# Decode attention of an MLA layer: scores in four 32-column strips over two key groups, and a new order of scoring and summing

## The chip, the cores and the metric

The kernel runs on one core of one Trainium2 chip. The metric is the device time of one execution in microseconds (us). The kernel before took 1875.65 us as the median of three runs (1873.12, 1875.65 and 2126.9). The execution that the profiler recorded took 1877.48 us, with a span of 1875.5 us.

## What is computed

One inference step of a two-layer decoder trunk. Layer 0 mixes tokens by multi-head latent attention (MLA), layer 1 by dilated sliding windows; each is followed by a squared-ReLU MLP. There are 512 prompt tokens and 8 samples (decode) with one new token each. The change touches only the MLA attention of the samples:

```python
# per sample: 16 heads, 4096 past keys in 32 pages, a latent of 256 and a rotary key of 32 each
ckv_past = ckv_pool[page_table].reshape(B, past, 256)
kpe_past = kpe_pool[page_table].reshape(B, past, 32)
q_lat = einsum("bthn,chn->bthc", q_nope, w_uk)
s_past = einsum("bthc,bkc->bhtk", q_lat, ckv_past) + einsum("bthr,bkr->bhtk", q_pe, kpe_past)
s_new  = einsum("bthc,bkc->bhtk", q_lat, c_kv) + einsum("bthr,bkr->bhtk", q_pe, k_pe)
p = softmax(concatenate([s_past, s_new]) * 96 ** -0.5)
o_lat = einsum("bhtk,bkc->bthc", p[..., :past], ckv_past) + einsum("bhtk,bkc->bthc", p[..., past:], c_kv)
o = einsum("bthc,chv->bthv", o_lat, w_uv) @ w_o      # after this the residual and the MLP
```

## The kernel before, in words

The program is written by hand, one instruction stream for each engine, tied by counting semaphores. Each engine takes its instructions strictly in the written order, so a wait holds back all that stands behind it. `dve.wait_ge` and the like are such waits; `link` makes VectorE wait for its own last result.

**Gathering.** The 4096 past keys of a sample are NG = 4 groups of 1024 keys. GpSimd fetches each with two indirect DMAs (L1941 the latents, 1 MB; L1942 the rotary keys), row p of a group holding 8 consecutive keys. The buffer `gat` has GR = 8 places, two samples. From group n = 8 on, the issue waits for `group_summed >= n - 7`: the same place must have been used by the sum of two samples earlier.

**Turning.** `turn_group` (L1311): VectorE transposes a group in blocks of 32x32 into `KT`, which has KR = 3 slots. A slot is free when the group that held it has been scored.

**Scores.** In a turned group, partitions 32i to 32i+31 hold 32 latent components of the keys of partition block i. `score_group` (L660, L661) multiplies with `qbd`, a block-diagonal weight matrix of 128x128 for each of 8 latent slices and the rotary slice: block i holds the 16 heads in the first 16 of its 32 columns, the rest are zeros. Nine matmuls of 256 columns give 128 x 256 scores of one group; two PSUM banks hold a sample's four groups. ScalarE fills `qbd` for two samples ahead (`spread_queries`, L1759, L1760).

**Softmax.** `key_max` (L1316 to L1322): VectorE reduces 128x1024 scores, brings the four blocks' maxima to partitions 0 to 31, takes the maximum with the new token's score and writes the bias for all blocks. ScalarE takes the exponentials with their row sums (L1771). `turn_probs` (L1330) turns 128x1024 probabilities back into blocks of 32 columns.

**Sums.** `sum_keys` (L671): 32 matmuls with 32 probability columns as weights, in turn in four column strips of the array (`r = 32 * (c % 4)`), 256 latent columns moving; the four strips' partial sums lie in four partition blocks. ScalarE copies them (L1779), `sum_rows` and `weights` make the denominators, `turn_latent` (L688, L689) adds the strips, divides and transposes, `latent_out` adds the new token.

**Order.** TensorE, for b = 0 to 8: score groups 0 and 1 of sample b; sum and row sums of b-1; score groups 2 and 3 of b; turn_latent of b-1. VectorE in each round: maximum of b-1, turn group 2 of b, turn the probabilities of b-1, turn groups 3 of b and 0 of b+1, weights of b-1, turn group 1 of b+1, latent of b-1. After the last sample TensorE multiplies with `w_uv` (L710), and the output projection with `w_omla` follows in four chunks, each split into a high and a low part by ScalarE (L1640) and GpSimd (L1901). The first two chunks are already in their raw buffer `wraw` during the decode attention; `KT` and `qbd0` lie in the place of the split buffer `whl`. SP issues all plain DMAs: `w_uv` waits for the seventh sum (`group_summed >= 28`).

## Time and profile before

| | before |
|---|---|
| profiled execution | 1877.48 us, span 1875.5 us |
| TensorE busy in the span | 1627.6 us (87%) |
| VectorE, ScalarE, GpSimd busy | 741.7, 450.1, 615.5 us |
| granted TensorE clock, mean of the span | 0.907 |
| first turned key group, first output projection | 390.17 us, 589.78 us |

"Busy" counts the time in which an engine works on an instruction; queue and semaphore instructions are left out. Matmul spans overlap, so a busy TensorE is not one at its peak. PEclk is the clock granted to TensorE as a share of 2.4 GHz: 0.50 is 1.2 GHz. A float32 matmul shows as two instructions. In brackets behind a row stands the idle time before it and who ended it. Idle time of an engine off the critical path costs nothing.

### The profile page before, as it was taken

How to read it: one execution, taken by the hardware profiler on the slowest of the kernel's cores; microseconds unless marked ns; L12 is line 12 of the kernel's file. 1: busy time of each engine (PE TensorE's matmuls, PEld its weight loads, DVE VectorE, ACT ScalarE, POOL GpSimd, SP SyncE). 2: the span in 40 equal slices, each digit the busy share in tenths (PEclk: the TensorE clock that was granted, in tenths of full speed). 3: DMA queues.
4: the chain of work that ended last, by engine and by line, in shares of the span. 5: the costliest groups of instructions: out<-in, count | busy, mean ns of one | idle time of the engine just before them, and what ended most of it. 6: DMA issues, size and time to landing. Idle time of an engine off the chain costs nothing.

```text
span 1875.5 us, 28456 instructions
## 1 busy us (share of the span) xinstructions
PE 1627.6 (87%) x12089; PEld 1514.2 (81%) x12089; DVE 741.7 (40%) x1156; ACT 450.1 (24%) x822; POOL 615.5 (33%) x277
## 2 busy tenths in 40 slices
PE   4657888679996999999999999998667999999995
PEld 3646666567776999999999999997545999999994
DVE  5355565366662542014312266313445641024114
ACT  3203343321112322112222111112432321122220
POOL 1311110313322464346533343221001464356440
PEclk8867788779998999999999999987876999999997
DMA  4125420235551453444433446445910453444221
GB/s 132 64 97 198 153 68 23 92 133 210 221 198 46 135 179 135 161 153 157 157 113 138 162 162 220 166 156 178 312 72 0 135 179 134 151 156 154 102 67 45
DMA packets 123259, 258.52 MB, mean 138 GB/s; under 512 B 7032, under 2 KB 104456, under 8 KB 116832
## 3 DMA queue, kind: packets, MB, share of 16 engines
q1 hardware_dynamic: 117024, 219.47, 34.3%
q0 software_dynamic: 6144, 37.75, 5.3%
q8 instruction: 68, 1.11, 0.2%
q14 instruction: 23, 0.19, 0.0%
HBM read 249.61 MB, written 95.58 MB: 184 GB/s over the span
## 4 chain that ended last, share of the span: by engine, by line
PE 73%; DVE 16%; DMA 3%; issue 2%; ACT 2%; POOL 2%; SPq 1%; ACTq 0%; DVEq 0%; POOLq 0%
PE ps L438 19%; PE ps L442 18%; PE ps L439 18%; PE ps L660 4%; PE ps L671 2%; DVE KT L1311 1%; PE ps L587 1%; PE ps L605 1%; DMA dv<-in_state 1%; PE ps L864 1%; DVE sq L1434 1%; PE ps L787 1%; DVE mxs L1261 1%; PE ps L830 1%; PE ps L661 1%
## 5 line engine op out<-in xcount | busy, mean ns | idle before, releaser
L1901 POOL TENSOR_TENSOR whl<-wraw,whl 128x2048 fp32r<-128x2048 f32 (+3 forms) x127 | 448.3, 3539 | 728.8 <-ACT whl L1640 728.7
L438 PE MATMUL ps<-hA,whl 128*128 128x260 f32 x1344 | 372.6, 296 | 43.0 <-POOL hA L1901 15.6
L439 PE MATMUL ps<-hA,whl 128*128 128x260 f32 x1344 | 365.8, 292 | 0.0
L1640 ACT ACTIVATE whl<-wraw 128x2048 fp32r<-128x2048 f32 (+3 forms) x127 | 185.9, 1487 | 499.0 <-PE ps L442 410.3
L438 PEld LDWEIGHTS ps<-hA,whl 128*128 128x128 f32 x1344 | 267.0, 199 | 46.7 <-POOL hA L1901 17.3
L438 PE MATMUL ps<-uT,whl 128*128 128x260 f32 x1024 | 273.5, 288 | 16.8 <-POOL uT L1901 16.8
L442 PE MATMUL ps<-hA,whl 128*128 128x260 f32 x1344 | 281.5, 292 | 0.0
L439 PE MATMUL ps<-uT,whl 128*128 128x260 f32 x1024 | 271.0, 285 | 0.0
L439 PEld LDWEIGHTS ps<-hA,whl 128*128 128x128 f32 x1344 | 267.7, 199 | 0.1
L442 PEld LDWEIGHTS ps<-hA,whl 128*128 128x128 f32 x1344 | 217.3, 198 | 0.0
L438 PEld LDWEIGHTS ps<-uT,whl 128*128 128x128 f32 x1024 | 196.9, 192 | 17.6 <-issue 17.6
L442 PE MATMUL ps<-uT,whl 128*128 128x260 f32 x1024 | 210.1, 287 | 0.0
L439 PEld LDWEIGHTS ps<-uT,whl 128*128 128x128 f32 x1024 | 197.3, 193 | 0.0
L1379 DVE TENSOR_TENSOR xT<-xT,ps 128x520 f32<-128x520 f32 (+1 forms) x48 | 33.4, 696 | 391.6 <-PE ps L442 391.3
L438 PE MATMUL ps<-hB,whl 128*128 128x260 f32 x640 | 168.8, 285 | 0.0
L439 PE MATMUL ps<-hB,whl 128*128 128x260 f32 x640 | 166.6, 282 | 0.0
L442 PEld LDWEIGHTS ps<-uT,whl 128*128 128x128 f32 x1024 | 160.4, 192 | 0.0
L442 PE MATMUL ps<-hB,whl 128*128 128x260 f32 x640 | 129.9, 285 | 0.0
L1901 POOL TENSOR_TENSOR uT<-tmp,uT 128x520 f32 x64 | 84.0, 1313 | 133.9 <-ACT uT L1650 133.9
L660 PE MATMUL ps<-KT,qbd 128*128 128x256 f32 x512 | 120.1, 389 | 9.0 <-DVE KT L1311 9.0
L1398 DVE SCALAR_TENSOR_TENSOR tmp<-ps,rstd 128x520 f32<-128x520 f32 x64 | 44.8, 700 | 199.8 <-PE ps L442 195.0
L439 PEld LDWEIGHTS ps<-hB,whl 128*128 128x128 f32 x640 | 121.6, 190 | 0.1
(255 smaller groups left out, 2139.6 us busy)
## 6 DMA issues: line engine op xcount, KB each, us to landing
out_ds<-in_state SPq DMA_DIRECT2D x32, 2047.0 KB, 10.5
wraw<-in_w_up SPq DMA_DIRECT2D x32, 1024.0 KB, 5.6
wraw<-in_w_down SPq DMA_DIRECT2D x32, 1024.0 KB, 5.1
wraw<-in_w_qkv SPq DMA_DIRECT2D x18, 1024.0 KB, 7.0
out_ds<-in_state SPq DMA_DIRECT2D x8, 2044.0 KB, 13.2
dv<-in_state SPq DMA_DIRECT2D x36, 256.0 KB, 5.8
dv<-q_scratch SPq DMA_DIRECT2D x6, 1024.0 KB, 7.3
wraw<-in_w_omla SPq DMA_DIRECT2D x4, 1024.0 KB, 5.4
```

The costliest lines, as they stand in the source:

```text
L438: pe.matmul(ps[:, 2 * u + a, 0:HALF], hi(k), rhs(k, 0)[:, c], start=first, stop=False)
L439: pe.matmul(ps[:, 2 * u + a, 0:HALF], hi(k), rhs(k, 1)[:, c], start=False, stop=False)
L442: ins = pe.matmul(ps[:, 2 * u + a, 0:HALF], lo(k), rhs(k, 0)[:, c], start=False, stop=last)
L587: pe.matmul(ps[:, i % 2, 0:(t + 1) * P], qh[:, h % 4, tok], kh[:, h % 4, 0:(t + 1) * P], start=True, stop=True).then_inc(scores_ready, 1)
L605: ins = pe.matmul(ps[:, 4 + i % 2, 0:VD], pT[:, i % 2, b * P:(b + 1) * P], v[:, b, h * VD:(h + 1) * VD], start=(b == 0), stop=(b == t))
L660: pe.matmul(out, qbd[b % 2][:, j, :], kt[:, :, j, :], start=(j == 0), stop=False)
L661: pe.matmul(out, qbd[b % 2][:, 8, :], KT[:, n % KR, KPP * KVL:], start=False, stop=True).then_inc(keys_scored, 1)
L671: ins = pe.matmul(ps[r:r + 32, 4 + b % 2, 0:KVL], pturn[:, c * 32:(c + 1) * 32], gat[:, n % GR, (c % KPP) * KVL:(c % KPP + 1) * KVL], star ...
L1379: free(dve.tensor_tensor(cols(xT, f), cols(xT, f), zt(u), ALU.add))
L1398: free(dve.scalar_tensor_tensor(out=out, in0=zt(u), scalar=0.0, in1=rooted(u), op0=ALU.max, op1=ALU.mult))
L1640: ins = act.activation(dst(0), src, ACT.Copy)
L1901: return pool.tensor_tensor(dst, src, hi.bitcast(F32), ALU.subtract)
```

## The change

- Scores of two groups are taken together: `qbd` has two stationary blocks of 32 columns for each slice (strip 0: heads of partition blocks 0 and 1, strip 1: of 2 and 3, 16 columns each); group g's strips go to partitions 64g and 64g+32. 36 matmuls a pair, one PSUM bank for a sample (128x512).
- The maximum runs over 128x512 and then over two halves of 16 heads, with two 32x32 transposes.
- The probabilities are turned 128x512 wide, and four ScalarE copies place them with zeros between them in `pfin`, from which the sums read as before.
- KR = 4: the fourth slot for turned keys is the first raw weight buffer `wraw[:, 0]` with a piece of `rstd`. The second `w_omla` chunk, which lay there, is loaded after all pairs are scored.
- A new order on TensorE, VectorE and ScalarE. The gathers on GpSimd and their waits are unchanged (GR = 8).

```diff
-KR = 3
+KR = 4
-        KT = sb("KT", [P, KR, GW], F32, cx)
-        qbd0 = sb("qbd0", [P, 9, P], F32, cx)
+        KT = sb("KT", [P, KR - 1, GW], F32, cx)
+        qbd = [sb(f"qbd{i}", [P, 9, 2, 32], F32, cx) for i in range(2)]
...
+        NB = 2 * KPP * 32
+        pexp = flat[:, 0:NB]
+        pturn = flat[:, NB:2 * NB]
+        pfin = flat[:, 2 * NB:4 * NB]
+        def keyT(n):
+            if n % KR < KR - 1:
+                return KT[:, n % KR, 0:KPP * KVL], KT[:, n % KR, KPP * KVL:]
+            return wraw[:, 0, :], rstd[:, T - KPP * ROPE:]
... TensorE
-            def score_group(n):
...
+            def score_pair(b, pair):
+                if pair == 0:
                     pe.wait_ge(queries_spread, b + 1)
                     if b >= 2:
                         pe.wait_ge(keys_exp, b - 1)
+                n0 = b * NG + 2 * pair
+                pe.wait_ge(keys_turned, n0 + 2)
+                for j in range(9):
+                    for g in range(2):
+                        ckv_, kpe_ = keyT(n0 + g)
+                        moving = ckv_.rearrange("p (s j q) -> p s j q", s=KPP, j=8)[:, :, j, :] if j < 8 else kpe_
+                        for st in range(2):
+                            r = 32 * (2 * g + st)
+                            ins = pe.matmul(ps[r:r + 32, b % 2, 256 * pair:256 * pair + 256], qbd[b % 2][:, j, st, :], moving,
+                                            start=(j == 0), stop=(j == 8), skip_group_check=True)
+                ins.then_inc(pairs_scored, 1)
             def sum_keys(b):
-                pe.wait_ge(probs_turned, b + 1)
+                pe.wait_ge(probs_placed, b + 1)
...
+            score_pair(0, 0)
+            score_pair(0, 1)
             for b in range(NS + 1):
-                if b < NS:
-                    score_group(NG * b)
-                    score_group(NG * b + 1)
                 if b:
                     sum_keys(b - 1)
                     sum_rows(b - 1)
-                if b < NS:
-                    score_group(NG * b + 2)
-                    score_group(NG * b + 3)
+                if b < NS - 1:
+                    score_pair(b + 1, 0)
+                    score_pair(b + 1, 1)
                 if b:
                     turn_latent(b - 1)
... SP
-            chunk((0, (KC, MC), wsrc(io["w_omla"], 0, KC, MC, MC)))
...
             sp.wait_ge(group_summed, NG * (NS - 1))
             sp.dma_start(wuv, wsrc(io["w_uv"], 0, 2, 0, H * VD)).then_inc(wuv_in, 16)
+            sp.wait_ge(pairs_scored, NS * NG // 2)
+            chunk((0, (KC, MC), wsrc(io["w_omla"], 0, KC, MC, MC)))
... VectorE
-            dve.memset(qbd0[:], 0.0)
-            dve.memset(qbd1[:], 0.0)
+            for t in (*qbd, mcol, mtop):
+                dve.memset(t[:], 0.0)
...
+            dve.memset(pfin, 0.0)
...
             def turn_group(n):
-                if due(n - KR + 1):
-                    dve.wait_ge(keys_scored, n - KR + 1)
+                if n >= KR:
+                    dve.wait_ge(pairs_scored, (n - KR) // 2 + 1)
+                elif n == KR - 1:
+                    dve.wait_ge(chunk_low, 5 + H // 2)
                 dve.wait_ge(gather_in[n % GR], 32 * (n // GR + 1))
-                dve.transpose(KT[:, n % KR, :], gat[:, n % GR, :]).then_inc(keys_turned, 1)
+                if n % KR < KR - 1:
+                    dve.transpose(KT[:, n % KR, :], gat[:, n % GR, :]).then_inc(keys_turned, 1)
+                else:
+                    ckv_, kpe_ = keyT(n)
+                    dve.transpose(ckv_, gat[:, n % GR, 0:KPP * KVL])
+                    dve.transpose(kpe_, gat[:, n % GR, KPP * KVL:]).then_inc(keys_turned, 1)
             def key_max(b):
...
-                link(dve.tensor_reduce(mall[:], mq[:, b, :], AX, ALU.max))
+                link(dve.tensor_reduce(mcol[:, 0:1], mq[:, b, :], AX, ALU.max))
+                link(dve.transpose(mrow[:], mcol[:]))
+                link(dve.tensor_tensor(mtop[0:1, :].rearrange("p (q h) -> p q h", q=2), two(mrow[0:1, 0:H]), two(mrow[0:1, H:2 * H]),
+                                       ALU.max))
+                link(dve.transpose(mrow[:], mtop[:]))
...
             def turn_probs(b):
                 dve.wait_ge(keys_exp, b + 1)
                 if b:
-                    dve.wait_ge(group_summed, NG * b)
+                    dve.wait_ge(probs_placed, b)
                 dve.transpose(pturn, pexp).then_inc(probs_turned, 1)
...
+            for n in range(4):
+                turn_group(n)
+            for b in range(NS + 2):
+                more = b < NS - 1
+                if more:
+                    turn_group(NG * b + 4)
+                    turn_group(NG * b + 5)
                 if b < NS:
+                    key_max(b)
+                if more:
+                    turn_group(NG * b + 6)
+                if b < NS:
+                    turn_probs(b)
+                if b >= 2:
+                    latent_out(b - 2)
+                if more:
+                    turn_group(NG * b + 7)
+                if 1 <= b <= NS:
+                    weights(b - 1)
... ScalarE, after the exponentials of b
                 if b + 2 < NS:
                     spread_queries(b + 2)
-                act.wait_ge(group_summed, NG * (b + 1))
+                act.wait_ge(probs_turned, b + 1)
                 if b:
-                    act.wait_ge(latent_ready, b)
-                act.activation(latent, ps[:, 4 + b % 2, 0:KVL], ACT.Copy).then_inc(latent_copied, 1)
+                    act.wait_ge(group_summed, NG * b)
+                for g in range(2):
+                    for q in range(2):
+                        dst = pfin[64 * q:64 * q + 64, :].rearrange("p (k g s h) -> p k g s h", k=2, g=2, s=KPP)[:, :, g, :, 0:H]
+                        src = pturn[64 * g:64 * g + 64, :].rearrange("p (k s h) -> p k s h", k=2, s=KPP)[:, :, :, H * q:H * (q + 1)]
+                        ins = act.activation(dst, src, ACT.Copy)
+                ins.then_inc(probs_placed, 1)
+                if b:
+                    latent_copy(b - 1)
+            latent_copy(NS - 1)
...
```

`latent_copy(b)` is the old copy with its two waits. The output of row sums and of turn_latent moves to PSUM banks 2, 3, 6 and 7; the `heads` constant sums over 16 instead of 32 partitions apart.


## Rows read from the trace of the kernel before

**Rows 1.** The page, part 4: chain that ended last, by line, share of the span.

```profile
PE ps L438 19%; PE ps L442 18%; PE ps L439 18%; PE ps L660 4%; PE ps L671 2%; DVE KT L1311 1%; PE ps L587 1%; PE ps L605 1%; DMA dv<-in_state 1%; PE ps L864 1%; DVE sq L1434 1%; PE ps L787 1%; DVE mxs L1261 1%; PE ps L830 1%; PE ps L661 1%
```

**Rows 2.** Windows: us; busy (x) of PE, PEld, DVE, ACT, POOL; PEclk, DMA share, GB/s.

```profile
440.00:460.00 20.00, 18.39 (x134) 14.47 (x133) 12.52 (x19) 1.97 (x7) 7.58 (x8) 1.00 0.62 237
```

**Rows 3.** Timeline, TensorE: start, us, line, operation, tiles, shapes, count; scores' start times.

```profile
445.69 3.70 PE L660 MATMUL ps<-KT,qbd 128*128 128x256 f32 x16
...
449.65 3.62 PE L660 MATMUL ps<-KT,qbd 128*128 128x256 f32 x16
...
455.37 3.72 PE L660 MATMUL ps<-KT,qbd 128*128 128x256 f32 x16
```

**Rows 4.** Line L671 in windows around samples 0, 2, 4, 6, 7: ns min/median/max, start times.

```profile
L671 PE MATMUL ps<-gat,tmp x64: 379/379/403, 419.4 to 422.7; 128*32 128x256 f32 x64
...
L671 PE MATMUL ps<-gat,tmp x64: 379/379/403, 464.3 to 467.6; 128*32 128x256 f32 x64
...
L671 PE MATMUL ps<-gat,tmp x64: 379/379/403, 509.2 to 512.5; 128*32 128x256 f32 x64
...
L671 PE MATMUL ps<-gat,tmp x64: 379/379/403, 554.0 to 557.3; 128*32 128x256 f32 x64
...
L671 PE MATMUL ps<-gat,tmp x64: 379/634/636, 572.5 to 577.8; 128*32 128x256 f32 x64
```

**Rows 5.** Timeline, GpSimd: first and last of the eight gather issues after sample 1's sum.

```profile
443.23 0.95 POOL L1941 DMA_INDIRECT gat<-in_ckv_pool,idx  x1 [12.73 <-PE ps L671]
...
451.99 0.95 POOL L1942 DMA_INDIRECT gat<-in_kpe_pool,idx  x1 [0.30 <-issue]
```

**Rows 6.** Line L1942, the small gather (kpe): time to landing over all 32.

```profile
DMA to landing us min/median/max: 5.5/7.4/8.3
```

**Rows 7.** Timeline, VectorE: turns of keys that waited for a gather (samples 4 and 6's).

```profile
473.17 2.58 DVE L1311 STREAM_TRANSPOSE KT<-gat 128x2304 f32<-128x2304 f32 x1 [6.42 <-DMA gat<-in_kpe_pool,idx]
...
516.70 2.58 DVE L1311 STREAM_TRANSPOSE KT<-gat 128x2304 f32<-128x2304 f32 x1 [5.07 <-DMA gat<-in_kpe_pool,idx]
```

**Rows 8.** Waits over 385 to 600 us: engine, line, waited for: us, times, longest.

```profile
DVE KT L1311 <- DMA gat<-in_kpe_pool,idx: 34.4, 6, 7.0
```

**Rows 9.** Timeline, VectorE: first turn; then key turn, latent, maximum, key turn, probabilities.

```profile
390.17 2.57 DVE L1311 STREAM_TRANSPOSE KT<-gat 128x2304 f32<-128x2304 f32 x1
...
454.84 2.58 DVE L1311 STREAM_TRANSPOSE KT<-gat 128x2304 f32<-128x2304 f32 x1 [1.92 <-PE ps L661]
...
457.35 0.14 DVE L1347 COPY pnb<-ps 128x16 f32<-128x16 f32 x1
...
457.81 1.22 DVE L1316 TENSOR_REDUCE mx<-ps 128x1 f32<-128x1024 f32 x1
...
460.53 2.58 DVE L1311 STREAM_TRANSPOSE KT<-gat 128x2304 f32<-128x2304 f32 x1
...
463.03 1.20 DVE L1330 STREAM_TRANSPOSE tmp<-tmp 128x1024 f32<-128x1024 f32 x1
```

**Rows 10.** Timeline, ScalarE: a query copy and a latent copy.

```profile
441.06 0.43 ACT L1759 ACTIVATE qbd<-sq 32x128 f32<-32x128 f32 x1
...
450.45 0.38 ACT L1779 ACTIVATE rstd<-ps 128x256 f32<-128x256 f32 x1 [8.84 <-remote]
```

**Rows 11.** Windows, columns as in rows 2: the granted clock before, in and after idle time.

```profile
396.00:399.00 3.00, 3.00 (x9) 2.33 (x8) 1.66 (x1) 0.00 (x0) 0.00 (x0) 0.50 0.52 216
...
568.00:570.00 2.00, 0.00 (x0) 0.00 (x0) 1.59 (x10) 0.19 (x1) 0.00 (x0) 0.93 0.00 0
...
570.00:572.00 2.00, 0.00 (x0) 0.00 (x0) 0.78 (x1) 1.19 (x3) 0.00 (x0) 0.50 0.00 0
...
574.00:576.00 2.00, 2.00 (x28) 0.85 (x21) 0.00 (x0) 0.00 (x0) 0.00 (x0) 0.50 0.00 0
```

**Rows 12.** DMA issues over 380 to 600 us: count, KB each, median us to landing.

```profile
wraw<-in_w_omla SPq DMA_DIRECT2D x2, 1024.0 KB, 5.9
```

**Rows 13.** Timeline, GpSimd: its half of the first two w_omla chunks.

```profile
580.49 8.96 POOL L1901 TENSOR_TENSOR whl<-wraw,whl 128x2048 fp32r<-128x2048 f32 x2 [37.82 <-ACT whl L1640]
```

More of the change, by code:

```diff
@@ L304, in program @@
         probs_turned = semaphore("probs_turned")
+        probs_placed = semaphore("probs_placed")
         group_summed = semaphore("group_summed")
@@ L655, in score_group @@
                         pe.wait_ge(keys_exp, b - 1)
-                pe.wait_ge(keys_turned, n + 1)
-                out = ps[:, 2 * (b % 2) + g // 2, (g % 2) * 256:(g % 2) * 256 + 256]
-                kt = KT[:, n % KR, 0:KPP * KVL].rearrange("p (s j q) -> p s j q", s=KPP, j=8)
-                for j in range(8):
-                    pe.matmul(out, qbd[b % 2][:, j, :], kt[:, :, j, :], start=(j == 0), stop=False)
-                pe.matmul(out, qbd[b % 2][:, 8, :], KT[:, n % KR, KPP * KVL:], start=False, stop=True).then_inc(keys_scored, 1)
+                n0 = b * NG + 2 * pair
[9 more added lines that the diff above has]
+                ins.then_inc(pairs_scored, 1)
             def sum_keys(b):
-                pe.wait_ge(probs_turned, b + 1)
+                pe.wait_ge(probs_placed, b + 1)
                 if b >= 2:
@@ L670, in sum_keys @@
                     n = b * NG + c // KPP
-                    ins = pe.matmul(ps[r:r + 32, 4 + b % 2, 0:KVL], pturn[:, c * 32:(c + 1) * 32],
+                    ins = pe.matmul(ps[r:r + 32, 4 + b % 2, 0:KVL], pfin[:, c * 32:(c + 1) * 32],
                                     gat[:, n % GR, (c % KPP) * KVL:(c % KPP + 1) * KVL], start=(c < 4), stop=(c >= NG * KPP - 4))
@@ L678, in sum_rows @@
                 pe.wait_ge(rows_ready, b + 1)
-                c = (b % 2) * 64
-                pe.matmul(ps[:, 6, c:c + 1], heads[:], rows[:, b % 2:b % 2 + 1], start=True, stop=True).then_inc(key_den_ready, 1)
+                pe.matmul(ps[:, 2 + b % 2, 0:1], heads[:], rows[:, b % 2:b % 2 + 1], start=True, stop=True).then_inc(key_den_ready, 1)
             def turn_latent(b):
@@ L685, in turn_latent @@
                 pe.wait_ge(latent_copied, b + 1)
-                c = (b % 2) * 64 + 8
                 for k in range(2):
-                    pe.matmul(ps[:, 6, c + k * H:c + (k + 1) * H], latent[:, k * P:(k + 1) * P], pick[:], start=True, stop=True)
-                pe.matmul(ps[:, 6, c + 2 * H:c + 3 * H], ones[0:32, :], dnew[:], start=True, stop=True).then_inc(latent_ready, 1)
+                    pe.matmul(ps[:, 6 + b % 2, k * H:(k + 1) * H], latent[:, k * P:(k + 1) * P], pick[:], start=True, stop=True)
+                pe.matmul(ps[:, 6 + b % 2, 2 * H:3 * H], ones[0:H, :], dnew[:], start=True, stop=True).then_inc(latent_ready, 1)
+            score_pair(0, 0)
+            score_pair(0, 1)
             for b in range(NS + 1):
-                if b < NS:
-                    score_group(NG * b)
-                    score_group(NG * b + 1)
                 if b:
@@ L1758, in spread_queries, with latent_copy @@
                     r = slice(32 * i, 32 * i + 32)
-                    act.activation(qbd[b % 2][r, 0:8, 32 * i:32 * i + H], qrep[r, :, :, b], ACT.Copy)
-                    ins = act.activation(qbd[b % 2][r, 8, 32 * i:32 * i + H], qpe[r, :, b], ACT.Copy)
+                    c = slice(H * (i // 2), H * (i // 2 + 1))
+                    act.activation(qbd[b % 2][r, 0:8, i % 2, c], qrep[r, :, :, b], ACT.Copy)
+                    ins = act.activation(qbd[b % 2][r, 8, i % 2, c], qpe[r, :, b], ACT.Copy)
                 ins.then_inc(queries_spread, 1)
+            def latent_copy(b):
+                act.wait_ge(group_summed, NG * (b + 1))
+                if b:
+                    act.wait_ge(latent_ready, b)
+                act.activation(latent, ps[:, 4 + b % 2, 0:KVL], ACT.Copy).then_inc(latent_copied, 1)
             spread_queries(0)
@@ L1998, in constants @@
         "half": halves.reshape(P, 2 * P),
-        "heads": (i[:, None] % 32 == i[None, :] % 32).astype(np.float32),
+        "heads": (i[:, None] % H == i[None, :] % H).astype(np.float32),
         "sel": (i[None, :] // 16 == np.arange(8)[:, None]).astype(np.float32),
```

55 lines of the change are left out of this document (17 added, 38 removed).

## The prediction, made before the changed kernel was run

> **What bounds the kernel now.** I read the page first. The chain that ended last is mostly TensorE, but the lines of this change hold few per cent of it: 4 and 1 for the scores (L660, L661), 2 for the sums (L671), 1 for the turning of keys (L1311) [rows 1]. All edits act in the decode attention, so I read that stretch by windows. In its middle TensorE is busy 18.4 us in 20 at full clock, VectorE 12.5, GpSimd's issues 7.6, and the gathers move 237 GB/s [rows 2]: here TensorE is the bound. The timeline says with what: one group's scores start every 3.96 us (449.65 - 445.69), in 18 instructions of 128x256, two to a float32 matmul; turn_latent then holds the next scores back until 455.37, 1.8 us [rows 3]. The sums of samples 0 and 6 start at 419.4 and 554.0, so a sample takes 134.6 / 6 = 22.4 us; the last sum starts 18.5 us later [rows 4].
>
> A second loop does not bind yet. The gather buffer has eight places, two samples: a group of sample b+1 is fetched once the same place has been summed for sample b-1. So every sum starts a burst. That of sample 1 starts at 419.4 + 22.4 = 441.8; GpSimd's first issue follows at 443.23, the eighth ends at 452.94, one every 1.25 [rows 5]. The first keys are turned 8.9 us after their sum (473.17 - 464.3), in another sample 7.5 (516.70 - 509.2) [rows 4, 7]; six such waits cost VectorE 34.4 us [rows 8]. Today's order hides this: two of four score groups come after the sum, and TensorE has work while the next keys land.
>
> **The change part by part.**
>
> *Strips.* A pair of groups now takes 36 matmuls of 32 columns (72 instructions) in four strips, instead of 36 instructions of 128. Their rate is on show: a sum is 64 instructions with 32-column weights in the same four strips, its starts spread over 3.3 us (419.4 to 422.7), 0.0525 us each; the full-width ones take 3.96 / 18 = 0.22 [rows 3, 4]. A pair costs 71 x 0.0525 + 0.38 = 4.1 us instead of 7.9, a sample 8.2 instead of 15.8. On the path throughout, this would shorten the stage by some 60 us.
>
> By the Trainium skill ("TensorE: Matmul & The Clock Gate", Measured speedup vs the span model) three column strips gave 2.38x, not 3x. At that efficiency four give 3.2x and a pair takes 5.3 us, an estimate, and the sum below would be 7 us higher. The row of the sums shows 4.2x (0.22 / 0.0525), and I go by the row.
>
> *Order.* TensorE now runs: sum b-1, both pairs of b+1, turn_latent b-1, sum b. So all four groups of b+1 must be gathered, turned and scored between sum b-1 and sum b, and their gathers start only with sum b-1; TensorE has nothing else meanwhile. VectorE is in order too: it turns two groups, takes the maximum of b, turns the third, turns the probabilities, writes the latent of b-2, turns the fourth. From the start of sum b-1:
> - First group in: 8.0, between 7.5 and 8.9. Turned in 2.5 (454.84 to 457.35): 10.5 [rows 7, 9].
> - Second group: its small gather is issued two and a half later than the first's (443.23 + 3.75 = 446.98) and takes 7.4 at the median: in at 12.6 after the sum; without any wait it would be 10.5. I take 11.5, the middle. Turned: 14.0 [rows 5, 6].
> - Maximum of b: now 2.7 (457.81 to 460.53). The reduction halves (-0.5 of 1.22). Added are two 32x32 transposes and a tiny maximum, which the trace lacks: bounds nothing and 0.17 each (the small copy of 457.35, start to start); I take the latter, as they are of its size, +0.5. So 2.7: 16.7 [rows 9].
> - Third group: in by 449.48 + 7.4, 15.1 after the sum, no wait: 19.2 [rows 5, 6].
> - Probabilities turned, half as wide: 0.65 instead of 1.20; the latent of b-2, 0.46 (457.35 to 457.81). 20.3 [rows 9].
> - Fourth group, in two instructions: 2.5, a second fixed part of 0.1 and the hand-over, 2.7. It is in by 451.99 + 8.3, 18.5, no wait. 23.0 [rows 5, 6, 9].
> - Second pair: 27.1. turn_latent: 1.8. The next sum starts at **28.9** [rows 3].
>
> That is 6.5 us more than today's 22.4, for the sums of samples 1 to 6: **+38.8 us**. With every term at its short end the period is 27.4, at its long end 30.8.
>
> *Placing the probabilities.* Four ScalarE copies of 64x256: 0.38 (128x256) to 0.43 each (32x128, strided) [rows 10], 1.7 in all. They start near 20.6, when the query copies are done, and end near 22.3; the second pair and turn_latent, up to 28.9, cover them. In the last sample that cover is gone and they stand in the sum, as below.
>
> *Start.* VectorE begins turning at 390.17 [rows 9]. Four turns come first, and the first pair waits for two of them: 395.2. TensorE is then at half clock (0.50 from 396 to 399 [rows 11]), so the pair takes 6 to 8 us, until 402. VectorE goes on: two turns 407.2, maximum 409.9, third turn, probabilities, fourth turn 416.0; second pair of sample 1 until 420.2. First sum at 420.3 against 419.4: **+0.9**. Of the memsets, half of the queries' goes and one of 128x1024 comes, about the same size.
>
> *End.* Sample 7 has no successor. Its scores end 1.7 before sum 6. Then maximum 2.7, exponentials about 1.0 (one tiny, one of twice the 256 columns that take 0.38 [rows 10]), turning 0.7; the copies wait for sum 6 (3.8) and take 1.7; the latent copy and turn_latent of 6 still come first: sum 7 starts 7.5 after sum 6, instead of 18.5: **-11.0**. And sum 7 has no long idle time before it now: today it takes 5.6 us, partly at half clock, then 3.7: **-1.9** [rows 4, 11].
>
> *The moved load.* The second w_omla chunk now leaves SP behind the wait for the seventh sum, after w_uv. A megabyte lands in 5.9 us [rows 12]; two one after the other are in 15.5 after sum 6 starts. ScalarE would come to split that chunk at 13.4 and wait 2.1, but GpSimd is then within its half of the chunk before (8.96 for two [rows 13]) and needs it at about 16.5: nearly nothing. If that cover is gone it costs up to 2.1. No transfer behind it on SP is due sooner. The new PSUM columns and the narrower new-token product cost nothing: the same small instructions at the same places.
>
> Sum: 38.8 + 0.9 - 11.0 - 1.9 = **+27**. The profiled execution took 1877.5 (span 1875.5 and 2.0 around it), 1.8 over the median of the runs. So 1904 against it, 1903 as a median.
>
> **The rivals.**
> - *VectorE-bound (faster).* The keys are there whenever VectorE asks. Then a sample costs its work: 10.1 for keys, 2.7, 0.65, 0.5, and 0.5 for the weights: 14.5. Six times -7.9, -13 at the end, +1: 1818. It decides if the gather for b+1 lands before sum b-1 ends. For it: TensorE's and VectorE's work would both fit. Against: the keys land 8 us after the sum that lets them be fetched, in all six waits [rows 7, 8]. 6%.
> - *The clock (slower).* TensorE idles from 4.2 to 14.0 in each period. With TensorE idle the granted clock is still 0.93 over 568 to 570 but 0.50 (1.2 GHz) over 570 to 572, and the sum that begins at 572.5 runs at 0.50 over 574 to 576 [rows 11]. So the first pair starts at 1.2 GHz and takes up to 7.7; it ends by 21.7, before the fourth turn at 23.0, and hides. The idle time after it is short, and I expect the second pair at 2.4 GHz. If that is at 1.2 too: +3.6, turn_latent +0.5, period 33.0, six times +10.6, and -12: 1929. It decides if the clock is down at 23.0. For it: at 396 to 399 the clock was still down with TensorE busy for all 3 us. 15%. The Trainium skill says on the same page (HAM oscillation — how this bites in real kernels) that bursts with waits between are throttled again each time; the trace agrees for one burst, and by that rule this rival holds.
> - *Strips don't overlap.* Scores one after another at 0.22 an instruction make a pair 15.8 and the period 47: about 2035. Against: the sums [rows 4]. 2%.
>
> **How the numbers follow.** My forecast has 77%: period 27.4 to 30.8, so 1895 to 1916. About 1 in 6 of it lies above 1913, where 2% begins (2% is about what a measurement can tell from no change). Slower by over 2%: 0.12 + 0.15 + 0.02 = 0.29. Faster: 0.06. Within: 0.65. The range adds to my own case a landing up to 1.5 us sooner and the clock's case: 1886 to 1930.
>
> **What would show it.** Sums that start near 29 us apart and not 22; TensorE idle near 10 us after each; VectorE waiting for the small gather about 8 us after each sum's start; score instructions of 128x32 every 0.0525 us when warm; a granted clock under 0.9 over the stage; sum 7 some 7.5 us after sum 6. I am wrong if the keys of b+1 are in before sum b-1 ends, or if the period is 22 or less.

## The result, and the profile after

The changed kernel takes 1907.12 us as the median of four runs (1905.35 to 1909.62); the kernel before, on the same chip, 1874.38. The ratio is 1.0172, with a 95% interval of 1.0148 to 1.0195: slower by 1.7%. The ratio is taken over undisturbed runs; one of the four of the kernel before, 2126.9, was in a slower state and does not count in it. The forecast was 1903, a ratio of 1.015. The profiled execution took 1908.67 us, span 1906.8, 31.3 more than before. The granted clock fell from a mean of 0.907 to 0.886.

The page of the changed kernel, part 1, and part 4 by engine:

```profile
PE 1584.1 (83%) x12665; PEld 1451.5 (76%) x12665; DVE 741.0 (39%) x1191; ACT 460.6 (24%) x854; POOL 615.5 (32%) x277
...
PE 69%; DVE 17%; issue 5%; DMA 3%; POOL 2%; ACT 2%; SPq 1%; DVEq 0%; ACTq 0%; POOLq 0%
```

TensorE is busy 43.5 us less than before (1627.6), and the kernel is slower all the same. The work that the strips save was not what the end waited for any more.

The sums, the line that answers to [rows 4], read in windows around samples 0, 2, 6 and 7:

```profile
L685 PE MATMUL ps<-gat,tmp x64: 379/379/379, 421.1 to 424.4; 128*32 128x256 f32 x64
...
L685 PE MATMUL ps<-gat,tmp x64: 379/379/403, 477.7 to 481.0; 128*32 128x256 f32 x64
...
L685 PE MATMUL ps<-gat,tmp x64: 379/379/403, 593.5 to 596.8; 128*32 128x256 f32 x64
...
L685 PE MATMUL ps<-gat,tmp x64: 379/506/634, 600.5 to 605.5; 128*32 128x256 f32 x64
```

From the first sum to the seventh it is 172.4 us, 28.7 a sample, against 22.4 before. The eighth starts 7.0 after the seventh.

The waits of the changed kernel over 385 to 640 us (engine, line, waited for: us, times, longest) answer to [rows 8]:

```profile
DVE KT L1326 <- DMA gat<-in_kpe_pool,idx: 85.5, 10, 13.8
PE ps L673 <- DVE KT L1326: 72.2, 8, 11.4
...
PE ps L673 <- DVE rstd L1330: 21.3, 7, 4.3
```

VectorE waits 85.5 us for gathers, before 34.4. TensorE's scores wait 93.5 us for turned keys: 72.2 before the eight first pairs (one of them at the start), 21.3 before seven second ones.

One whole period, from the sum of sample 1 to the sum of sample 2, in the timeline of the changed kernel (start, us, engine, line, operation; in brackets the idle time before and who ended it):

```profile
449.19 3.66 PE L685 MATMUL ps<-gat,tmp 128*32 128x256 f32 x64
450.56 0.94 POOL L1977 DMA_INDIRECT gat<-in_ckv_pool,idx  x1 [18.37 <-PE ps L685]
...
456.63 2.58 DVE L1326 STREAM_TRANSPOSE KT<-gat 128x2304 f32<-128x2304 f32 x1 [13.56 <-DMA gat<-in_kpe_pool,idx]
...
459.49 2.58 DVE L1326 STREAM_TRANSPOSE KT<-gat 128x2304 f32<-128x2304 f32 x1 [0.28 <-issue]
461.99 0.65 DVE L1335 TENSOR_REDUCE mx<-ps 128x1 f32<-128x512 f32 x1
...
462.21 6.84 PE L673 MATMUL ps<-KT,qbd 128*32 128x256 f32 x72 [9.05 <-DVE KT L1326]
...
463.50 0.20 DVE L1341 STREAM_TRANSPOSE mrow<-mcol 32x32 f32<-32x32 f32 x1
...
464.84 2.58 DVE L1326 STREAM_TRANSPOSE KT<-gat 128x2304 f32<-128x2304 f32 x1
...
467.34 0.67 DVE L1354 STREAM_TRANSPOSE tmp<-tmp 128x512 f32<-128x512 f32 x1
...
468.04 1.70 ACT L1811 ACTIVATE tmp<-tmp 64x256 f32<-64x256 f32 x4
...
468.44 2.31 DVE L1329 STREAM_TRANSPOSE wraw<-gat 128x2048 f32<-128x2048 f32 x1
...
470.67 0.40 DVE L1330 STREAM_TRANSPOSE rstd<-gat 128x256 f32<-128x256 f32 x1
...
471.13 0.58 PE L673 MATMUL ps<-KT,qbd 128*32 128x256 f32 x2 [2.08 <-DVE rstd L1330]
...
476.84 0.62 PE L700 MATMUL ps<-pick,rstd 128*128 128x16 f32 x4
...
477.71 3.66 PE L685 MATMUL ps<-gat,tmp 128*32 128x256 f32 x64
```

Read it as a relay. GpSimd has waited 18.37 us for the sum; VectorE has waited 13.56 for the first keys; TensorE idles 9.05 before the first pair and 2.08 before the second. The next sum follows the second pair at once. Nobody waits for the four ScalarE copies of L1811.

Windows of the changed kernel, columns as in [rows 2]:

```profile
459.00:462.00 3.00, 0.00 (x0) 0.00 (x0) 2.72 (x3) 0.00 (x0) 0.97 (x2) 0.50 0.97 384
...
469.00:471.00 2.00, 0.05 (x4) 0.00 (x0) 2.00 (x3) 1.12 (x3) 0.00 (x0) 1.00 0.00 0
471.00:473.00 2.00, 1.87 (x20) 1.03 (x24) 0.55 (x4) 0.00 (x0) 0.00 (x0) 0.56 0.00 0
475.00:477.00 2.00, 2.00 (x38) 1.07 (x30) 0.00 (x0) 0.00 (x0) 0.00 (x0) 1.00 0.03 8
600.00:604.00 4.00, 4.00 (x45) 2.31 (x48) 0.56 (x3) 0.00 (x0) 0.00 (x0) 0.62 1.06 383
```

The clock is down while TensorE idles before the first pair (0.50). By the end of that pair it is up and it stays up in the idle time after it (1.00 over 469 to 471), falls again at the start of the second pair (0.56 over 471 to 473), and is up at that pair's end. The eighth sum meets the same fall (0.62). TensorE had idled 2.16 us shortly before it:

```profile
599.64 0.59 PE L700 MATMUL ps<-pick,rstd 128*128 128x16 f32 x4 [2.16 <-ACT rstd L1790]
```

### The profile page after: what moved, and what is told of

Same layout as the page of the kernel before. It is cut to its first block, busy times and chain, and to the rows that moved or that the text cites. A ratio compares the mean times of both kernels' runs of the same rounds, so it can differ in the third digit from the quotient of the medians.

```text
span 1906.8 us, 29683 instructions
## 1 busy us (share of the span) xinstructions
PE 1584.1 (83%) x12665; PEld 1451.5 (76%) x12665; DVE 741.0 (39%) x1191; ACT 460.6 (24%) x854; POOL 615.5 (32%) x277
## 4 chain that ended last, share of the span: by engine, by line
PE 69%; DVE 17%; issue 5%; DMA 3%; POOL 2%; ACT 2%; SPq 1%; DVEq 0%; ACTq 0%; POOLq 0%
PE ps L448 19%; PE ps L452 18%; PE ps L449 18%; DVE KT L1326 2%; PE ps L597 1%; PE ps L673 1%; PE ps L615 1%; DMA dv<-q_scratch 1%; DVE sq L1455 1%; DMA gat<-in_kpe_pool,idx 1%; PE ps L875 1%; PE ps L798 1%; DVE mxs L1272 1%; PE ps L841 1%; DVE wraw L1329 1%
## 5 line engine op out<-in xcount | busy, mean ns | idle before, releaser
L448 PE MATMUL ps<-hA,whl 128*128 128x260 f32 x1344 | 373.0, 297 | 43.5 <-POOL hA L1937 15.8
L673 PE MATMUL ps<-KT,qbd 128*32 128x256 f32 x864 | 86.7, 477 | 93.5 <-DVE KT L1326 72.2
L673 PEld LDWEIGHTS ps<-KT,qbd 128*32 128x32 f32 x864 | 44.1, 136 | 131.6 <-issue 94.4
```

Source lines behind the costliest of these rows:

```text
L448: pe.matmul(ps[:, 2 * u + a, 0:HALF], hi(k), rhs(k, 0)[:, c], start=first, stop=False)
L673: ins = pe.matmul(ps[r:r + 32, b % 2, 256 * pair:256 * pair + 256], qbd[b % 2][:, j, st, :], moving, start=(j == 0), stop=(j == 8), skip_g ...
```

## The experiments

Theory: a chain for each sample sets the period, namely sum, gather, four turns with the maximum and the probabilities between them, second pair, turn_latent. Its causes are the order of work and the eight gather places. Rivals: TensorE's own work, the clock, the strips. A "period" below is the distance of the first sum to the seventh, divided by six. Each time stands beside that of the kernel before on the same chip, which differs from chip to chip (1866.81 to 1875.61), so the ratios are what to compare.

**Which pair is on the path.** Samples 1 to 7 compute their first pair (twice0) or their second pair (twice1) a second time.

```diff
-                for j in range(9):
+                for j in [x for _ in range(2 if pair == 0 and b else 1) for x in range(9)]:    # twice0; twice1: pair == 1
```

> The first score pair of samples 1 to 7 is computed twice over (same result); nothing else changes. Theory (the sum of b-1, the gather of b+1, its turning, the second pair, the next sum form one chain, and the first pair lies beside the turning): the first pair grows from 5.5 to 6.8 us to 9.6 to 10.9 us in an idle time of about 9 us; it ends at most about 1 us after the fourth turn, and TensorE's clock is then up at the second pair, which gives back 1.7 us where it was down. So 1907 us, between 1900 and 1914. Rival (TensorE's own work or the strips set the period): each of 7 pairs adds 4.1 us, so 1936 us.

> The second score pair of samples 1 to 7 is computed twice over (same result). Theory (the second pair stands on the chain between the fourth turn and the next sum): 7 times 4.1 us, so +29 us, 1936 us. Rival (the period is set elsewhere, by VectorE's work or by the gathers alone, with the scores beside them): below 1915 us.

The sums of samples 0 and 6 in twice0:

```profile
L685 PE MATMUL ps<-gat,tmp x64: 379/379/379, 416.7 to 420.0; 128*32 128x256 f32 x64
...
L685 PE MATMUL ps<-gat,tmp x64: 379/379/403, 590.7 to 594.0; 128*32 128x256 f32 x64
```

and in twice1:

```profile
L685 PE MATMUL ps<-gat,tmp x64: 378/379/380, 424.3 to 427.6; 128*32 128x256 f32 x64
...
L685 PE MATMUL ps<-gat,tmp x64: 378/379/404, 623.4 to 626.7; 128*32 128x256 f32 x64
```

twice0 takes 1902.34 us against 1870.83 before, ratio 1.0164 [1.0127, 1.0201], period 29.0: the same as the changed kernel within the interval, though 72 more matmul instructions run in each of seven samples. twice1 takes 1937.76, 1.0353 [1.0323, 1.0384], period 33.2. Equal work, put at two places, costs 0.3 or 4.5 us a sample. The 0.3 is a net figure: the doubled first pair delays the second one to 0.3 to 1.8 us behind the fourth turn, and in return the second pair runs at full clock in all six periods (4.1 us), where the changed kernel has it so in two. So the first pair has slack for most of the added work, and the second is on the path. TensorE's amount of work is refuted as the bound.

**Is it the gathers.** The first eight groups alone are gathered, so that the keys always wait for VectorE. This kernel leaves out the other 24 groups and works on samples 2 to 7 with old keys.

```diff
-                dve.wait_ge(gather_in[n % GR], 32 * (n // GR + 1))
+                dve.wait_ge(gather_in[n % GR], 32)
-            for n in range(NS * NG):
+            for n in range(GR):
```

> Only the first eight key groups are gathered; later samples reuse what lies in the buffer, so the scores and sums of samples 2 to 7 are made from the wrong keys, with all other work unchanged. Theory (the landing of keys after each sum is the head of the chain): VectorE no longer waits for a gather, the period falls from 28.7 to VectorE's own work of about 15 us, between 14.9 and 16.5; six times -13.5: 1826 us, between 1815 and 1840. Rival (the slow part is the second pair, the clock or the copies, and the gather only seems to be waited for): at least 1890 us.

The sums of samples 0 and 6:

```profile
L685 PE MATMUL ps<-gat,tmp x64: 379/379/379, 421.0 to 424.3; 128*32 128x256 f32 x64
...
L685 PE MATMUL ps<-gat,tmp x64: 379/379/403, 507.1 to 510.4; 128*32 128x256 f32 x64
```

1823.93 us, ratio 0.9745 [0.9716, 0.9775], period 14.35. Half of the period is waiting for keys, not work. It is also the price that the prediction gave to its VectorE-bound rival (14.5 a sample): that rival's period was right and its condition does not hold. Its total, 1818, was 10 too low (0.9745 x 1875.65 = 1828).

**The clock.** TensorE multiplies 18 times 128x256 for nothing after the row sums and 8 times between the pairs, and so does not idle.

```diff
+            def keep_warm(b, count):
+                for _ in range(count):
+                    pe.matmul(ps[:, b % 2, 256:512], heads[:], dist[:, 0:256], start=True, stop=True, skip_group_check=True)
...
+                    if b:
+                        pe.wait_ge(keys_exp, b)
+                        keep_warm(b + 1, 18)
                     score_pair(b + 1, 0)
+                    if b:
+                        keep_warm(b + 1, 8)
                     score_pair(b + 1, 1)
```

> TensorE fills its idle time with matmuls whose results are never read: 18 of 128x256 after each sum's row sums (7.9 us), 8 between the first and the second pair (3.5 us), so that its clock stays at 2.4 GHz. Theory (the chain is a chain of latencies; the clock costs only what the second pair loses in it): the second pair takes 4.1 us in all six periods instead of 5.8 in four, so -7 us: 1900 us, between 1896 and 1905. Rival (the idle time's low clock is the cause of the slowdown against the kernel before): at or below 1885 us.

A window over one period (columns as in [rows 2]):

```profile
449.00:478.00 29.00, 26.00 (x290) 18.91 (x290) 14.29 (x26) 5.12 (x16) 7.55 (x8) 1.00 0.42 164
```

and the sums of samples 0 and 6:

```profile
L685 PE MATMUL ps<-gat,tmp x64: 378/379/380, 421.0 to 424.2; 128*32 128x256 f32 x64
...
L685 PE MATMUL ps<-gat,tmp x64: 378/379/403, 588.0 to 591.2; 128*32 128x256 f32 x64
```

The clock is 1.00 (in the changed kernel the same window has 0.76), all six second pairs take 4.10 us, and the period falls by 0.9 to 27.8. Two of the six first pairs still begin at a low clock (5.8 and 5.6 us). 1902.76 us, ratio 1.0152 [1.0119, 1.0184], whose interval overlaps that of the change. The clock is a small part of the period, as the forecast's main case had it.

**The number of places.** A ninth gather place, made of the second raw weight buffer and a tile for the rotary keys. One group of the next sample can then be fetched before the sum.

```diff
-GR = 8
+GR = 9
-        gat = sb("gat", [P, GR, GW], F32, cx)
+        gat = sb("gat", [P, GR - 1, GW], F32, cx)
+        kpe9 = sb("kpe9", [P, KPP * ROPE], F32, cx)
+        def place(n):
+            if n % GR < GR - 1:
+                return gat[:, n % GR, 0:KPP * KVL], gat[:, n % GR, KPP * KVL:]
+            return wraw[:, 1, :], kpe9[:]
... SP: the first w_omla chunk too is loaded after the seventh sum
```

> The changed kernel with nine gather places instead of eight: the ninth is the second raw weight buffer with a small tile, and the first w_omla chunk, which lay there, is loaded after the seventh sum. The first group of b+1 is then fetched a whole sample earlier, and the second one with the first group of sum b-1. Theory (the landing of keys heads the chain): from a sum's start, second group in 7.6, turned 10.1, maximum 13.0, third turn 15.5, probabilities and latent 16.8, fourth turn 19.4, second pair 23.5 to 25.2, turn_latent 24.3 to 26: period 24.3 to 26 instead of 28.7, so -16 to -26 us: 1881 to 1891 us where the kernel before takes 1874. Rival (DMA bandwidth or the second pair alone sets the period): above 1900 us.

The sums of samples 0 and 6 (of the latter, the three groups that lie in `gat`):

```profile
L692 PE MATMUL ps<-gat,tmp x64: 379/379/379, 417.8 to 421.0; 128*32 128x256 f32 x64
...
L692 PE MATMUL ps<-gat,tmp x48: 379/379/403, 565.3 to 568.5; 128*32 128x256 f32 x48
```

1883.29 us against 1875.61, ratio 1.0049 [1.0023, 1.0074], period 24.6: one place is worth 4.1 us a sample. The period had grown by 6.3; one buffer gives two thirds of that back. The second pair starts 19.1 us after the sum in the mean, instead of 22.7, which is 3.6 of the 4.1; the rest is clock (two second pairs of six take 5.8 us, not four).

**The order on VectorE.** With eight places, the maximum of b and the turning of its probabilities now come before the four turns of b+1 and so fall into the wait for the gather. early_max_nine has the ninth place as well.

```diff
-            for b in range(NS + 2):
-                more = b < NS - 1
-                if more:
-                    turn_group(NG * b + 4)
-                    turn_group(NG * b + 5)
...                  sample 0: turn_group(4), (5), key_max(0), turn_probs(0), turn_group(6), (7)
+            for b in range(1, NS + 2):
                 if b < NS:
                     key_max(b)
-                if more:
-                    turn_group(NG * b + 6)
...                  turn_probs(b), latent_out(b - 2), weights(b - 1)
+                if b < NS - 1:
+                    for g in range(4, 8):
+                        turn_group(NG * b + g)
```

> The changed kernel; on VectorE alone the maximum and the turning of the probabilities of b (with the latent of b-2 and the weights of b-1) now stand before the four turns of b+1, in the time in which it waits for their gather. TensorE's and ScalarE's orders stay. Theory (landing, four turns, second pair, turn_latent are one chain, and the maximum stands in it only through VectorE's order): first group in at 7.5, second about 11.3, third and fourth not before 14.3 and 17.3; fourth turned at 20.0, second pair 24.1 to 25.8, next sum 24.9 to 26.6, instead of 28.7: 6 times -3, so 1884 to 1895 us against 1907 of the changed kernel (ratio to the kernel before 1.006 to 1.012). Rival (the landing of the fourth group or DMA bandwidth sets the period): above 1900 us.

> early_max with the nine gather places of ninth_place. The first group of b+1 is in before the sum of b-1, the others at 7.6, 11.3, 14.3: fourth turned at 17.0, second pair 21.1 to 22.8, next sum 21.9 to 23.6, against 24.6 in ninth_place: 1868 us where the kernel before takes 1875, between 1860 and 1878; it would be the first to beat the kernel before or equal it. If TensorE's instructions come late during the burst, as in old_order, the first pair suffers, not the second, and little is lost.

The sums of samples 0 and 6 in early_max:

```profile
L685 PE MATMUL ps<-gat,tmp x64: 379/379/379, 421.9 to 425.1; 128*32 128x256 f32 x64
...
L685 PE MATMUL ps<-gat,tmp x64: 379/379/403, 572.4 to 575.7; 128*32 128x256 f32 x64
```

and in early_max_nine:

```profile
L692 PE MATMUL ps<-gat,tmp x64: 379/379/379, 422.2 to 425.4; 128*32 128x256 f32 x64
...
L692 PE MATMUL ps<-gat,tmp x48: 379/379/403, 554.4 to 557.7; 128*32 128x256 f32 x48
```

early_max: 1886.81 us against 1866.81, 1.0099 [1.007, 1.0129], period 25.1. Of the 3.6 us, 2.5 are chain: the second pair starts 20.2 us after the sum in the mean, instead of 22.7. That is less than the 3.5 that the maximum and the probabilities take (2.85 + 0.67), since VectorE now stands idle 0.3 to 0.9 us before the third and the fourth turn too, and in two periods the first pair ends after the fourth turn. The other 1.1 is clock: all six second pairs take 4.1 us, where four of six took 5.8. early_max_nine: 1867.14, 1.0002 [0.9979, 1.0025], period 22.0: with both, the whole loss is gone.

**The strips in the order of before.** TensorE, VectorE and ScalarE keep the sequence of the kernel before (pair, sum, pair, turn_latent), with strips, narrow maximum and placing as changed.

```diff
-            score_pair(0, 0)
-            score_pair(0, 1)
             for b in range(NS + 1):
+                if b < NS:
+                    score_pair(b, 0)
                 if b:
                     sum_keys(b - 1)
                     sum_rows(b - 1)
-                if b < NS - 1:
-                    score_pair(b + 1, 0)
-                    score_pair(b + 1, 1)
+                if b < NS:
+                    score_pair(b, 1)
                 if b:
                     turn_latent(b - 1)
```

> Strips, one bank a sample, placed probabilities and four slots kept; only the order on TensorE, VectorE and ScalarE is that of the kernel before (first pair of b, sum b-1, second pair of b, turn_latent b-1; VectorE as before). Theory (the new order is what costs, and with any order the strips can only give what the gather and VectorE's order leave): from a sum's start the first group of b+1 lands at 8, two turns and the weights end at 13.5, latent 14, maximum 16.9, third turn 19.4, probabilities 20.1, copies 21.8: period 22 instead of 22.4 of the kernel before and 28.7 of the changed one; the first sum 4 us earlier, the last one 4 us earlier than in the kernel before: 1864 us, between 1856 and 1872, where the kernel before takes 1874. Rival (strips, copies or the new maximum are what costs): 1890 us or more.

The sums of samples 0 and 6:

```profile
L685 PE MATMUL ps<-gat,tmp x64: 379/379/403, 414.9 to 418.1; 128*32 128x256 f32 x64
...
L685 PE MATMUL ps<-gat,tmp x64: 379/634/634, 564.6 to 570.7; 128*32 128x256 f32 x64
```

The scores' waits over 395 to 600 us (waited for: us, times, longest; "issue" is time in which the engine waited for nothing that the profile shows):

```profile
PE ps L673 <- issue: 14.7, 29, 0.8
```

Windows inside one second pair (445.67 to 455.14), in the burst of gathers, columns as before:

```profile
448.00:450.00 2.00, 1.44 (x6) 0.19 (x4) 1.65 (x1) 0.00 (x0) 1.62 (x2) 1.00 0.96 389
450.00:452.00 2.00, 1.25 (x6) 0.30 (x6) 1.47 (x4) 0.00 (x0) 1.21 (x2) 1.00 1.00 373
...
454.00:456.00 2.00, 2.00 (x33) 1.47 (x27) 0.79 (x1) 0.00 (x0) 0.00 (x0) 1.00 0.95 397
```

The theory missed: 22 us expected, 24.95 measured; 1892.18 us against 1875.61, 1.0099 [1.0075, 1.0122]. The second pair takes 9.5 us or more instead of 4.1. At full clock, with all keys turned, TensorE gets 6 matmul instructions in 2 us, where it later does 33. That later window has the same DMA share (0.95), so the share alone does not set the rate. What has ended by then is the issuing of the gathers on GpSimd, here its last issue and the first instruction at the full rate:

```profile
450.57 0.95 POOL L1975 DMA_INDIRECT gat<-in_kpe_pool,idx  x1 [0.30 <-issue]
...
453.16 0.42 PE L673 MATMUL ps<-KT,qbd 128*32 128x256 f32 x2 [0.81 <-issue]
```

The full rate comes back 1.64 us after the last issue ends (453.16 - 451.52). It does so 1.6 to 1.7 us after it in all six bursts of this run, and the gathers' packets go on for another 3.6 to 6 us. Besides, the sums have a median of 634 ns at the end and take 5 to 6.5 us, as TensorE now idles before them.

**The same fault elsewhere.** late_scores puts both pairs of b behind the sum of b-1; late_scores_warm adds 11 empty multiplications before each sum.

```diff
-            score_pair(0, 0)
-            score_pair(0, 1)
...
                     sum_rows(b - 1)
-                if b < NS - 1:
-                    score_pair(b + 1, 0)
-                    score_pair(b + 1, 1)
+                if b < NS:
+                    score_pair(b, 0)
+                    score_pair(b, 1)
... VectorE: weights(b-1), turn_group(4b+4), key_max(b), turn_probs(b), latent_out(b-1), three turns
... ScalarE: places the probabilities before it copies queries; latent_copy(b)
```

> The changed kernel with another order: TensorE runs sum b-1, both pairs of b, turn_latent b-1, sum b, so no sum waits for keys that were fetched after the sum before; VectorE turns one group of b+1, takes the maximum of b, turns the probabilities of b at once, then turns the other three groups; ScalarE places the probabilities before it copies queries. From a sum's start: both pairs end at 12.4, maximum 15.3, exponentials 16.4, probabilities 17.1, copies 18.8: the next sum. The first key group lands at 8 and lies beside the pairs. Theory: period 18.8 with the clock up; TensorE idles some 5 us ahead of each sum, so a sum and part of a pair may run at half clock, up to 20.8. First sum 7 us earlier than in the kernel before: 1846 to 1858 us where that takes 1874. Rival (the gathers' landing sets the period in any order): 1885 us or more.

> As late_scores, with 11 matmuls of 128x256 (4.8 us, results never read) in TensorE's idle time ahead of each sum. If the clock is what late_scores loses, the period is 18.8 and the time 1846 us; if TensorE is at 2.4 GHz there anyway, nothing changes against late_scores, or it gets slower where the extra matmuls delay a sum (up to 1 us a sample).

The same wait in late_scores:

```profile
PE ps L673 <- issue: 16.8, 30, 1.0
```

and a window of late_scores within a first pair:

```profile
462.00:464.00 2.00, 1.17 (x8) 0.43 (x8) 0.43 (x3) 0.38 (x1) 1.39 (x3) 1.00 1.00 416
```

late_scores: 1901.9 us against 1875.61, 1.0154 [1.0094, 1.0215], period 27.0 where 18.8 to 20.8 was expected; the two pairs take 12.8 to 16 us together instead of 8.2. late_scores_warm: 1896.74, 1.0114 [1.0058, 1.017], period 26.0, the pairs still 14.6 to 17.0. The clock is not the main cause: with 1.00 through the whole pair, a first pair still took 10.6 and 10.8 us, and the gaps come at full clock. In both runs, too, the full rate returns 1.6 to 1.7 us after GpSimd's last issue in every burst.

**Gathers or not.** old_order once more, with the edit of resident (the groups after the eighth are left out).

> old_order with only the first eight key groups gathered (later samples use the wrong keys; all other work unchanged). In old_order the second pair of b ran in 9.5 to 10.3 us instead of 4.1, in waits that the profile calls issue, while the gathers held the DMA engines. Theory (TensorE's instructions, four times as many for each us as with full-width scores, are fetched late while the gathers fill the DMA engines, and its clock falls with it): no gathers, no such waits, the second pair takes 4.1 to 5.8 us, and the period is VectorE's and the copies' chain, 17.5 us instead of 24.9: 1840 to 1852 us. Rival (the strips in this place are slow by themselves, or by the low clock alone): a second pair of 8 us or more, period above 21 us, 1865 us or more.

A window over exactly one second pair:

```profile
418.30:422.40 4.10, 4.10 (x74) 2.30 (x74) 3.07 (x4) 0.25 (x1) 0.00 (x0) 1.00 0.02 6
```

The second pairs take 4.10 us, and the waits hold no "issue" of the scores any more. 1853.7 us against 1866.81, 0.9931 [0.9903, 0.9959], period 19.2 (17.5 expected; the sums still run at half clock, 5 us and more). So it is the gathers that hold back the narrow scores. The edit takes away their issuing on GpSimd together with their traffic, and no run parts the two; the moments above point to the issuing, since the gaps end with it and not with the packets. How it acts is open. The wide scores of the kernel before lie in the same burst and are not disturbed; its window with a DMA share like that:

```profile
446.00:454.00 8.00, 7.70 (x37) 6.46 (x35) 3.23 (x4) 0.38 (x1) 5.41 (x6) 1.00 0.98 383
```

Those 72 instructions in 8 us (9 a us) are more than the 10 and 12 in 2 us (5 to 6 a us) above, so a plain ceiling on instructions per time does not explain it. That strips use up instructions four times as fast per us of work, and that their supply comes late in such a burst, is an argument, not shown. In the changed kernel itself every first pair begins 1.9 us or more after the last issue, so this fault does not touch its scores.

**A last try.** early_max_nine with turn_latent of b-1 between the two pairs of b+1, and sample 0 summed before sample 1 is scored.

```diff
+            sum_keys(0)
+            sum_rows(0)
+            score_pair(1, 0)
+            score_pair(1, 1)
+            for b in range(1, NS + 1):
...
                     score_pair(b + 1, 0)
+                turn_latent(b - 1)
+                if b < NS - 1:
                     score_pair(b + 1, 1)
-                if b:
-                    turn_latent(b - 1)
... VectorE and ScalarE follow: the maximum and the probabilities of sample 0 come before groups 5 to 7
```

> early_max_nine, with two more things taken out of the chain. turn_latent of b-1 runs between the two pairs of b+1, in TensorE's idle time, instead of after the second pair: 0.8 us less a period, 21.2 to 22.0. At the start, sample 0 is summed before sample 1 is scored, so that the first burst of gathers starts at about 412 instead of 422 us; sample 1's sum then starts at about 441 instead of 443.7, since its own four turns and the maximum of sample 1 still follow. Theory: 7 us less than early_max_nine (ratio 1.000 to the kernel before): ratio 0.996, between 0.994 and 0.999. Rival (TensorE's clock or late instructions in the pairs eat it): 1.000 or more.

1869.04 us against 1868.45, 1.0009 [0.9992, 1.0026]. Missed: 7 us were expected, and the output projection comes 1.7 us earlier than in early_max_nine. From the second to the seventh sum the period is 21.9 us against 22.1, a gain of 0.2 and not 0.8, and the eighth sum takes 5.1 us instead of 3.7, at a clock of 0.71. No version here that gathers all keys beats the kernel before.

## Why the prediction was right

The forecast said 1903 (range 1886 to 1930) by way of a period of 28.9; measured were 1907 and 28.7. The loop is right as to its mechanism. That the period agrees to 0.2 us is in part luck, as two errors in it cancel. Its steps, against the period of the timeline above, in us after the start of the sum:

| step, done at | predicted | measured |
|---|---|---|
| first group in | 8.0 | 7.4 (456.63 - 449.19) |
| second group's turn starts | 11.5 | 10.3 (459.49) |
| third turn starts (maximum takes 2.7; 2.85) | 16.7 | 15.7 (464.84) |
| fourth turn starts | 20.3 | 19.3 (468.44) |
| second pair starts | 23.0 | 21.9 (471.13) |
| second pair done | 27.1 | 27.7 |
| next sum | 28.9 | 28.5 (477.71) |

This period is one of six, which run from 27.1 to 30.8 us. The spread comes from the wait for the second group, whose turn starts 10.3 to 12.6 us after the sum, and from the clock of the second pair, which starts 21.5 to 24.2 us after the sum, 22.7 in the mean (forecast 23.0).

- **The loop.** Right: the sum frees the places, and the keys come 7.4 to 8.0 us later. resident shows it by taking the gathers away (14.35), ninth_place by adding a place (24.6), early_max by shortening the chain (25.1; 1.1 of the gain of 3.6 is clock).
- **Maximum, probabilities, fourth turn.** Right within 0.2 each. The two 32x32 transposes and the tiny maximum, which the trace of before lacked, were put at 0.5 and take 0.68 (463.50 to 464.18); the maximum's total was taken as 2.7 and is 2.85.
- **Strips.** Right: a pair at full clock takes 4.10. The prediction's estimate of 5.3, from the Trainium skill's figure for three strips ("TensorE: Matmul & The Clock Gate", Measured speedup vs the span model), does not hold here: every unhindered pair at full clock took 4.1.
- **Second pair's clock.** Sized wrongly, and this is where the rival of the clock holds in part. The forecast had it at 2.4 GHz. In four of six periods it took 5.8 us and in two 4.1, 5.2 in the mean: +1.1. In those four the clock was up in the idle time before the pair and fell within its first 1.4 us. The idle times were 2.08, 2.91, 3.33 and 3.41 us; after 2.45 and 2.79 us it stayed up, so their length does not tell which. The price was 1.7 and not 3.6, since the clock came up within the pair. The Trainium skill ("TensorE: Matmul & The Clock Gate", HAM oscillation — how this bites in real kernels) describes bursts that start slow again after each wait for a DMA. The trace agrees for the first pairs: all six took 5.5 to 6.8 us, after 9.05 us of idle time in the timeline above. For the second pairs it does so in four periods of six.
- **turn_latent.** Sized wrongly: 0.8 (476.91 to 477.71), not 1.8. In the kernel before it lies in the burst of gathers, and its timeline there shows two gaps marked "issue" of the kind that old_order made many of; in the changed kernel it lies behind the burst, without them. This error (-1.0) and the clock's (+1.1) nearly cancel in each period. The rows of before:

```profile
454.00 0.27 PE L688 MATMUL ps<-pick,rstd 128*128 128x16 f32 x1 [0.30 <-issue]
454.71 0.41 PE L688 MATMUL ps<-pick,rstd 128*128 128x16 f32 x3 [0.44 <-issue]
```

- **Start** +1.7 (421.1 against 419.4) for +0.9, because sample 1's second pair ran at a low clock too. **Sums 1 to 6** +37.8 (172.4 - 134.6) for +38.8. **End** -11.5 (7.0 for 18.5) for -11.0.
- **The eighth sum's clock.** This term failed. It was to be warm, -1.9; it takes 5.35 us (600.48 to 605.84, clock 0.62) against 5.62, so -0.3. TensorE idles 2.16 us before it as well, and the clock falls as above.
- **The moved load and the copies.** Nearly nothing, right: from the eighth sum's start to the first output projection it is 17.1 us (617.6 - 600.5), before 17.3 (589.8 - 572.5).

Together the projection starts 27.8 us later (617.6 for 589.8), and +27 was forecast. The span grew by 31.3. The other 3.5 us arise after the stage, in the dilated layer between 1171 and 1301 us; the variants show it too (1288 to 1290 us from the first output projection's inputs to the end, one 1293; 1286.1 before). Its cause was not studied and stays open.

## What to carry to other kernels

Making the busiest engine's work cheaper helps only as far as no loop closes behind it: look for the event that frees a buffer, add up what must happen from there until the same event comes again, and compare with that engine's work. When an order is changed, count what now stands inside that loop; here one more buffer place was worth 4.1 us a sample, and moving the maximum and the probabilities into the wait 3.6, of which about 1.1 came from the clock. A place in time has a price of its own: the same pair took 4.1 us after the gathers' issuing and 9.5 us or more within it. Doubling the suspected work at one place of the loop and then at another tells which side bounds it.

## What the runs showed of the hardware

- Narrow score instructions came at 6 in 2 us instead of 33 while GpSimd was issuing indirect gathers (old_order, DMA share 0.96 to 1.00), and the wait is marked "issue". The full rate came back 1.6 to 1.7 us after the last issue in all 18 bursts of old_order, late_scores and late_scores_warm, with the DMA share still near 1 (0.95 at 33 instructions in 2 us). Without gathers the same pair took 4.10 us. The 128-column scores in the same burst were not hindered, short instructions (turn_latent, 16 columns moving) a little: gaps of 0.30 and 0.44 us.
- After 2.1 to 3.4 us of idle time between two pairs the clock, still 1.00 in the idle time, fell to 0.50 within the first 1.4 us of the second pair, in four periods of six; in one of the four the idle time was 2.08 us.
- Empty multiplications held the clock at 1.00 over one whole period (449 to 478), not over all six, and won 0.9 us of 28.7.
